# A decoder stack on one core: the third block of each MLP's first product by seven quarter products, with its weight sums on GpSimd

## The reference, cut to what matters

```python
def rms_norm(x, g):
    y = x * lax.rsqrt(jnp.mean(x * x, axis=-1, keepdims=True) + NORM_EPS)
    return y * g

def sqrelu_mlp(x, w1, w2):          # x 512 x 1024, w1 1024 x 4096, w2 4096 x 1024
    h = jax.nn.relu(x @ w1)
    return (h * h) @ w2
```

## Time and profile before

| | us |
|---|---|
| median of 3 runs | 1942.14 (1940.47 to 1942.18) |
| the profiled execution | 1938.0 |
| its span, first to last instruction | 1936.2 |
| TensorE busy | 1909.1 (99% of the span) |
| VectorE busy | 1364.7 (70%) |
| ScalarE busy | 913.6 (47%) |
| GpSimd busy | 243.6 (13%) |

### The profile page before, as it was taken

How to read it: one execution, slowest core, us unless ns; L and a number is a source line. 1 busy time by engine, 2 the same in 40 slices (tenths; PEclk the granted TensorE clock), 3 DMA queues, 4 the chain that set the end, 5 groups by cost and what they waited for, 6 DMA issues and landing times.

```text
span 1936.2 us, 29515 instructions
## 1 busy us (share of the span) xinstructions
PE 1909.1 (99%) x12066; PEld 1623.7 (84%) x12066; DVE 1364.7 (70%) x1899; ACT 913.6 (47%) x1366; POOL 243.6 (13%) x319
## 2 busy tenths in 40 slices
PE   9999999999999999999999999999999999999998
PEld 7877889899888876678899988887798788899897
DVE  5448587776775678857777776778765567777775
ACT  4227453433443688854343343676653444433432
POOL 3100000000002137620000000075400200000001
PEclk9999999999999999999999999999999999999999
DMA  6320223233234440013223223231143132233231
GB/s 205 103 92 3 88 90 107 87 110 109 88 109 131 151 132 2 2 45 109 88 90 114 102 87 112 90 109 55 53 144 132 44 109 88 88 109 109 88 109 66
DMA packets 30928, 181.36 MB, mean 94 GB/s; under 512 B 4752, under 2 KB 7824, under 8 KB 10320
## 3 DMA queue, kind: packets, MB, share of 16 engines
q1 hardware_dynamic: 28000, 172.68, 26.3%
q0 software_dynamic: 1952, 6.03, 1.1%
q10 hardware_dynamic: 848, 0.83, 0.1%
HBM read 172.72 MB, written 2.10 MB: 90 GB/s over the span
## 4 chain that ended last, share of the span: by engine, by line
PE 93%; DVE 3%; issue 1%; ACT 1%; POOL 1%; DMA 1%; DVEq 0%; POOLq 0%; ACTq 0%
PE ps L578 28%; PE ps L579 28%; PE ps L580 28%; PE ps L2017 2%; PE ps L1185 1%; PE ps L1975 1%; PE ps L1249 1%; PE ps L1225 1%; DVE n_probs L2121 1%; POOL f_probs L1907 1%; DVE f_probs L1798 0%; DMA x_res<-in_xT 0%; PE ps L1964 0%; PE ps L2014 0%; PE ps L1409 0%
## 5 line engine op out<-in xcount | busy, mean ns | idle before, releaser
L578 PE MATMUL ps<-o_hi,w_hi 128*128 128x512 f32 (+1 forms) x1032 | 403.4, 391 | 0.0
L579 PE MATMUL ps<-o_lo,w_hi 128*128 128x512 f32 (+1 forms) x1032 | 400.8, 388 | 0.0
L580 PE MATMUL ps<-o_hi,w_lo 128*128 128x512 f32 (+1 forms) x1032 | 400.3, 388 | 0.0
L547 ACT ACTIVATE w_hi<-w_raw 128x2048 fp32r<-128x2048 f32 x109 | 208.7, 1915 | 272.3 <-PE ps L580 271.3
L578 PE MATMUL ps<-h_hi,w_hi 128*128 128x512 f32 (+2 forms) x896 | 318.4, 355 | 1.5 <-DVE w_lo L557 0.9
L580 PE MATMUL ps<-h_hi,w_lo 128*128 128x512 f32 (+2 forms) x896 | 316.1, 353 | 0.0
L579 PE MATMUL ps<-h_lo,w_hi 128*128 128x512 f32 (+2 forms) x896 | 316.0, 353 | 0.0
L564 DVE TENSOR_TENSOR w_lo<-w_raw,w_hi 128x2048 fp32r<-128x2048 f32 x109 | 254.9, 2339 | 62.6 <-ACT w_hi L547 62.4
L580 PEld LDWEIGHTS ps<-o_hi,w_lo 128*128 128x128 f32 x1032 | 193.9, 188 | 40.1
L578 PEld LDWEIGHTS ps<-o_hi,w_hi 128*128 128x128 f32 x1032 | 194.0, 188 | 39.9 <-issue 1.5
L579 PEld LDWEIGHTS ps<-o_lo,w_hi 128*128 128x128 f32 x1032 | 194.1, 188 | 38.2 <-issue 0.5
(11 more groups left out here) (363 smaller groups left out, 3556.9 us busy)
## 6 DMA issues: line engine op xcount, KB each, us to landing
w_raw<-in_wstream SPq DMA_DIRECT2D x159, 1024.0 KB, 4.8
x_res<-in_xT SPq DMA_DIRECT2D x4, 512.0 KB, 4.6
out_T<-x_res SPq DMA_DIRECT2D x5, 256.0 KB, 2.4
e_cmp<-kv_nat POOLq DMA_DIRECT2D x8, 128.0 KB, 6.4
k_slc<-kv_nat POOLq DMA_DIRECT2D x8, 128.0 KB, 5.0
k_win<-kv_nat POOLq DMA_DIRECT2D x8, 128.0 KB, 7.5
mem_in<-in_memT POOLq DMA_DIRECT2D x1, 1024.0 KB, 5.1
e_cmp<-kv_nat POOLq DMA_DIRECT2D x8, 127.8 KB, 7.0
```

What stands on the lines that cost most here:

```text
L547: act.activation(w_hi[:, par, :, :], w_raw[:, par, :, :], ACT.Copy).then_inc(hi_ready, 1)
L578: pe.matmul(o, l_hi, r_hi, start=first, stop=False)
L579: pe.matmul(o, l_hi, r_lo, start=False, stop=False)
L580: return pe.matmul(o, l_lo, r_hi, start=False, stop=last)
```

## The change

Three things are changed, in each of the three MLPs.

1. `PLAIN` goes from 3 to 2, so slot 2 is a seven slot too. The order of hidden and output slots stays (`LEAD`, `PAIRED`).
2. For slot 2 alone, the four `sum_raw` sums (`raw_sums`) and the low parts of the plain quarters (`plain_lows`) are made by GpSimd in a new `pool_mlp`. GpSimd starts the sums when the block has landed, and the low parts when slot 0's tiles are done and ScalarE has made the high parts. VectorE keeps the two `sum_lo` subtractions of slot 2 and now waits for `plain_ready` ahead of the last.
3. The token work is earlier in the order. On VectorE `token_difference` stands ahead of `vector_root` in slot 0, `token_sums` ahead of the work on slot 2's weights, and `tokens_low` directly behind that, ahead of `hidden_low(0)` and of the evacuation of slot 1. On ScalarE `gained` is in slot 0, slot 2's `sums` ahead of `hidden(0)`, and `tokens_high` behind it, one slot earlier.

```diff
-        PLAIN = 3
+        PLAIN = 2
         SEVENS = 16 - PLAIN
...
+        LEAD, PAIRED = 3, 13
+        HIDDEN = {slot: slot for slot in range(LEAD)}
+        HIDDEN.update({LEAD + 1 + 2 * n: LEAD + n for n in range(PAIRED)})
+        OUTPUT = {LEAD + 2 * v: v for v in range(PAIRED)}
...
+        def raw_sums(eng, n, raw, begin, end):
+
+            if begin == 0:
+                eng.tensor_tensor(sum_raw[:, 0, :, :], quarter(1, 0, raw), quarter(1, 1, raw), ALU.add).then_inc(sums_made, 1)
+                eng.tensor_tensor(sum_raw[:, 1, :, :], quarter(1, 0, raw), quarter(0, 0, raw), ALU.subtract).then_inc(sums_made, 1)
+                eng.wait_ge(sums_made, 4 * n + 1)
+                eng.tensor_tensor(sum_raw[:, 2, :, :], sum_raw[:, 0, :, :], quarter(0, 0, raw), ALU.subtract).then_inc(sums_made, 1)
+            if end == 4:
+                eng.wait_ge(sums_made, 4 * n + 3)
+                eng.tensor_tensor(sum_raw[:, 3, :, :], quarter(0, 1, raw), sum_raw[:, 2, :, :], ALU.subtract).then_inc(sums_made, 1)
+
+        def plain_lows(eng, n, raw, hi, lo):
+
+            eng.wait_ge(plain_high, 2 * n + 1)
+            eng.tensor_tensor(lo[:, 4:8, :], raw[:, 4:8, :], f32(hi[:, 4:8, :]), ALU.subtract)
+            eng.wait_ge(plain_high, 2 * n + 2)
+            eng.tensor_tensor(quarter(0, 0, lo), quarter(0, 0, raw), f32(quarter(0, 0, hi)), ALU.subtract).then_inc(plain_ready, 1)
+
+        def pool_mlp(pool, m):
+
+            blk = b["mlp%d" % m] + LEAD - 1
+            par, n = blk % 2, SEVENS * m
+            raw, hi, lo = (w[:, par, :, :] for w in (w_raw, w_hi, w_lo))
+            pool.wait_ge(split_ready, blk - 1)
+            pool.wait_ge(raw_landed[par], 16 * (blk // 2) + 16)
+            raw_sums(pool, n, raw, 0, 4)
+            pool.wait_ge(tile_done, 2 * blk - 2)
+            plain_lows(pool, n, raw, hi, lo)
...
                 if slot == 0:
                     scalar_root(act, name)
+                    gained()
...
+                if slot == 1:
+                    sums(slot + 1)
                 if slot - 1 in HIDDEN:
                     hidden(slot - 1)
-                if seven(slot + 1):
+                if slot == 1:
+                    tokens_high()
+                if slot > 1 and seven(slot + 1):
                     sums(slot + 1)
                 if seven(slot):
                     copy_product(slot)
-                if slot == 1:
-                    gained()
-                if slot == 2:
-                    tokens_high()
...
+                if slot > LEAD - 1:
+                    dve.wait_ge(raw_landed[par], 16 * (blk // 2) + 16)
+                    dve.wait_ge(tile_done, 2 * blk - 2)
+                    raw_sums(dve, n, raw, 0, 3)
+                    plain_lows(dve, n, raw, hi, lo)
+                    raw_sums(dve, n, raw, 3, 4)
                 dve.wait_ge(sums_high, n + 1)
                 dve.wait_ge(sums_made, 4 * n + 4)
                 dve.tensor_tensor(sum_lo[:, 0:3, :, :], sum_raw[:, 0:3, :, :], f32(sum_hi[:, 0:3, :, :]), ALU.subtract)
                 dve.wait_ge(hi_ready, blk + 1)
+                dve.wait_ge(plain_ready, n + 1)
                 dve.tensor_tensor(sum_lo[:, 3, :, :], sum_raw[:, 3, :, :], f32(sum_hi[:, 3, :, :]), ALU.subtract).then_inc(split_ready, 1)
...
+                if slot == 1:
+                    token_sums()
                 if seven(slot + 1):
                     sums_and_lows(slot + 1)
                 elif blk + 1 < NBLK:
                     vector_split(dve, blk + 1, (blk + 1) % 2)
                 if slot == 0:
+                    token_difference()
                     vector_root(dve, name)
-                    token_difference()
+                if slot == 1:
+                    tokens_low()
                 if slot - 1 in HIDDEN:
                     hidden_low(slot - 1)
-                if slot == 1:
-                    token_sums()
-                if slot == 2:
-                    tokens_low()
...
             pool_sb(pool)
+            pool_mlp(pool, 0)
             pool_compress(pool)
             pool_nsa(pool)
+            pool_mlp(pool, 1)
...
             pool_cross(pool)
+            pool_mlp(pool, 2)
             pool_final(pool)
```

More of the change, by code:

```diff
@@ L799, in build_program @@
         SLOTS = 32
-        PLAIN = 3
+        PLAIN = 2
         SEVENS = 16 - PLAIN
-        HIDDEN = {slot: slot for slot in range(PLAIN)}
-        HIDDEN.update({PLAIN + 1 + 2 * n: PLAIN + n for n in range(SEVENS)})
-        OUTPUT = {PLAIN + 2 * v: v for v in range(SEVENS)}
+        LEAD, PAIRED = 3, 13
+        HIDDEN = {slot: slot for slot in range(LEAD)}
+        HIDDEN.update({LEAD + 1 + 2 * n: LEAD + n for n in range(PAIRED)})
+        OUTPUT = {LEAD + 2 * v: v for v in range(PAIRED)}
         LATE = {SLOTS - 3 + n: parts for n, parts in enumerate(LATE_PARTS)}
```

## The result

The changed kernel takes 1948.9 us (median of 6 runs, 1946.57 to 1950.65), the kernel before, run beside it, 1940.36 (6 runs, 1939.62 to 1942.18). The ratio is 1.0043, with 95% bounds of 1.0033 and 1.0053: it is 0.43% slower, against a forecast of 1948.2. But the forecast counted 6.1 us of loss from a median of 1942.14; the loss is 8.5, from 1940.36. So 2.4 us of the loss are not in the forecast's sum.

A forecast was written before the change was run, and what follows sets the result against it. TensorE, busy 99% of the span, bounds the kernel; per MLP 2.85 us late less 0.81 saved is 2.04, 6.1 for three; 1938.0 + 6.1 = 1944.1, plus 4.1 for the median gives 1948.2, range 1943 to 1952.

The forecast's parts named there:

- VectorE's chain: VectorE's queue in slot 1, from slot 0's evacuation to tokens_low: tok_ready at 267.82, wanted at 265.15.
- The restart: TensorE loading weights and starting again after its slot 2 wait: 0.2 us taken, 0 to 0.5.
- The hold-up: VectorE two-SBUF-input instructions and GpSimd's SBUF reads lock each other out; the two low parts cost VectorE 3.34 us.
- Rival A: Slot 2: no hold-up, or low parts done in time; TensorE gains 0.81 three times, median 1939.7; chance 0.12.
- B: Slot 2: GpSimd's turns cost VectorE half, 1.7 us; net 0.4 per MLP, 1943.3 in all; chance 0.15.
- C: GpSimd dearer, 1.86 and 3.72 us, so 5.20 lost; net 3.9 per MLP, 1953.8 in all; chance 0.11.
- That delay costs nothing more: GpSimd's sums delay slot 0's hid_buf to 254.2 from 252.64, without further cost, the low part lying partly under it.
- the lower one: Forecast's lower bound: GpSimd at 1.04 and 2.08, no restart; 2.25 late, net 1.24 per MLP, 1945.8.
- Later slots: From slot 3 on, the order slots 4, 5 and 6 have now, TensorE never idle; free.
- the 1.3 us to spare: Slot 3: hid_ready comes 5.9 us after tok_ready, while TensorE still has 7.2 us of matmuls.
- rival D: Stalled TensorE gets the lower clock for one slot per MLP, some 10 us more each, 1978; chance 0.02.
- The base: Median of the kernel before, 1942.14, 4.1 above its profiled execution of 1938.0; the forecast loss was added to it.

The follow-up runs named there:

- the table of two by two: Changed kernel with GpSimd's sums and low parts each kept or replaced by memsets; tok_lo ends 263.8 with neither, 267.0 low parts only, 265.4 sums only, 267.7 both.
- on VectorE: Changed kernel with slot 2's four sums and two low parts made by VectorE, no GpSimd work in the MLPs; 1958.88 us, 1.0101 of the kernel before.
- low parts twice: Changed kernel with GpSimd making slot 2's two low parts twice over; 1962.78 us, 1.0119 of the kernel before.
- the changed kernel again: Changed kernel run once more with no edit, for a second profile; 1949.22 us, 1.0041 of the kernel before.
- no reads: Changed kernel with GpSimd's six slot 2 instructions replaced by memsets of zeros, so it reads nothing; 1938.04 us, 0.999 of the kernel before.
- the sums alone: Changed kernel with GpSimd's four sums kept and its two low parts filled with zeros by memset; 1937.85 us, 0.9989 of the kernel before.
- token work early: Changed kernel with slot 2's products reordered, token_difference and gained before the previous layer's last tile, low parts on VectorE; 1937.07 us, 0.9985 of the kernel before.
- old product order: The token work early kernel with slot 2's products back in the changed kernel's order; 1940.81 us, 0.9999 of the kernel before.
- products reordered: Changed kernel with slot 2's seventh product taken third, ahead of those reading tok_hi and tok_lo; 1942.49 us, 1.0007 of the kernel before.
- low parts alone: Changed kernel with GpSimd's two low parts kept and its four sums filled with zeros by memset; 1947.23 us, 1.0034 of the kernel before.

## Why the prediction was right, and where it was not

**VectorE's chain** came out as worked out. On the scale of the earlier trace rows, predicted and measured: the split of slot 1 done at 247.3 and 247.05, `token_difference` at 249.6 and 249.3, the reciprocal 252.9 and 252.5, `hid_buf` of slot 0 at 254.2 and 253.9, `token_sums` 261.05 and 261.07, `sum_lo` 263.33 and 263.34, `tok_lo` 267.82 and 267.74, the third product 2.85 late and 2.65 (270.48 - 2.68 - 265.15). The restart was 0.06, not 0.2. Net 1.84 for each MLP where 2.04 was forecast; by the stretches between the MLPs 1.97.

**The hold-up**, read from one place in another stage, is the right mechanism: GpSimd's reads off, and it is gone; twice the low parts, and it is there twice. Rival A (no hold-up) falls with it, as does B (half): VectorE paid in full. The prices too: 2.41 for GpSimd's 1024 elements against 2.43; 3.2 us for the pair against 3.34. C (dearer with the rounded output) is out. The estimate of 2.25 from the Trainium skill (GPSIMD Engine Reference, Elementwise — side-by-side cycle accounting) was under the 2.41 that was measured. The reciprocal was taken as free, and that was not put to the test, since GpSimd has a gap there; what reads PSUM is free in the trace (1.29 for 1.28).

**"That delay costs nothing more"** was wrong. The delay from the sums costs 0.7 us of the final wait, shown by the table of two by two. The sum of the chain came out all the same, 267.74 for 267.82, and that is luck: without the sums `token_sums` starts 0.4 before the 252.64 that I had added to (252.2: `token_difference` no longer stands between the reciprocal and the evacuation), and the low parts cost a little less than I took. Of the bounds, the lower one has a slip: "2.25 late" should be 2.85 - 0.60 - 0.20 = 2.05, and its net of 1.24 follows from that.

**Later slots** were as predicted: no wait in slots 3 and 4, and the 1.3 us to spare showed when the first wait was taken away (1.20 of wait at slot 3).

**The mis-sized term is the clock, rival D.** I gave 0.02 to the lower clock, at a price of 10 us for each MLP. The mechanism was right and common, the price was off: 1.5 to 2.3 us a time, in none, two or all three MLPs of an execution. (The stretches between the MLPs grew by 6.76, 6.02 and 6.10 us in the kernel on VectorE, where the wait accounts for 4.44, and by 7.33, 7.78 and 7.17 with the low parts twice, where it accounts for 5.55.) Both grounds that I had against it fail on their own rows. A slice of the page is 48.4 us long and its digit 9 means 90% or more, so a drop for 3.4 us (271.2 to 274.6 in the changed kernel again) leaves it at 9; the page of the kernel with the low parts twice, with a drop in all three MLPs, has forty nines as well. And the "waits of several us in the attention stages" are totals of many short ones. In the list of the kernel before, the longest single wait of TensorE is 1.8 us:

```profile
PE ps L1975 <- DVE n_min L2121: 6.2, 9, 1.1
...
PE ps L384 <- DVE nrm L345: 1.8, 1, 1.8
```

So that trace held no wait like the one that I forecast, and said nothing about what follows one.

How much of the loss is the clock's can be worked out in two ways. The first goes by what the waits leave over. TensorE's lateness in slot 2 or 3 is the listed idle time plus 0.16 (the changed kernel's 2.65 against 2.49: the idle time starts at the modelled end of the last matmul, 0.28 long where they start every 0.12), so the waits of three MLPs make the sum of the three latenesses, less 2.4. The second way goes by the mean granted clock that is on record for every run of a kernel, not for the profiled one alone: (1 - granted clock) times the span is the time that the lower clock takes away, and the last column has its mean over the runs, less the same for the runs of before beside them.

| kernel | idle, three MLPs | from waits | measured | left over | by the granted clock |
|---|---|---|---|---|---|
| no reads | 0 | -2.4 | -2.8 | -0.4 | -0.6 |
| the sums alone | 0.5 | -1.5 | -3.0 | -1.5 | -1.4 |
| token work early | 0 | -2.4 | -3.5 | -1.1 | -0.4 |
| old product order | 1.8 | -0.1 | 0.0 | 0.1 | -0.6 |
| products reordered | 3.6 | 1.7 | 1.7 | 0.0 | -0.2 |
| low parts alone | 5.3 | 3.4 | 6.4 | 3.0 | 2.7 |
| changed kernel | 7.5 | 5.6 | 8.4 | 2.8 | 2.1 |
| on VectorE | 15.3 | 13.4 | 18.3 | 4.9 | 7.2 |
| low parts twice | 18.6 | 16.7 | 22.2 | 5.5 | 9.1 |

Waits of up to 1.2 us leave nothing over, or up to 1.5 us less than nothing; waits of 1.8 and more leave 3 to 5.5 us. The two last columns agree within 0.7 us down to the changed kernel. In the last two rows the recorded clock is also low for a part of the wait itself, where it costs nothing: that part is 2.6 and 4.4 us in the two profiles, and without it 4.6 and 4.7 are left, for 4.9 and 5.5. So about 2 to 3 us of the changed kernel's 8.4 are the lower clock. In the profiles it lies behind each of the waits of 1.8, 5.1 and 6.2 us (three of three in one execution of each kernel) and behind two of six of those of 2.5. It was not more frequent with the longer of 1.8 and 2.5; what decides whether it comes is open.

**The base** was off in the other direction. I took the median of three runs, 1942.14; the six runs beside the changed kernel give 1940.36, and 26 runs 1940.8. A loss 2.4 too small on a base 1.8 too high made 1948.2 against 1948.9. That it lies closer than its parts is luck. The 2.4 are 8.5 - 6.1: the waits came out at 5.6 by the sum above (5.9 by the stretches), and the rest, 2.6 to 2.9, is about what the lower clock takes. A gain of the size of TensorE's can be told from nothing, too: ten or eleven executions of a kernel showed 2.8 to 3.5 us, where I had taken 3.9 as the least.

## What to carry to other kernels

Work moved to an idle GpSimd isn't off VectorE where it reads SBUF beside VectorE's instructions with two SBUF inputs: each GpSimd turn costs VectorE about its length (3.2 us for turns of 3.7), and no wait in the trace says so, only longer instructions. Whether the move pays depends on what it lies beside. The low parts, wholly beside `token_sums`, cost VectorE 3.2 us for work that it does itself in 1.7. The sums, which lie partly where VectorE waits for others, cost it 0.7 to 1.6 us, for four instructions of 0.6 us each. Price such a move by where it lies; and before moving work at all, see whether the order of the consumer can ask for it later. With a TensorE that is never idle, count a new stall of about 2 us as its length plus, in some executions, 1.5 to 2.3 us for the lower clock; before calling such a cost absent, see whether your trace holds a single stall of that length, since a total of short ones and a digit of the page don't show it. And take the base from many runs.

## What the runs showed of the hardware

That a TensorE busy for 98% of the span is granted 1.2 GHz after a single short wait was not expected: 8.79 in place of 7.28 us for 60 matmuls after 2.5 us of idle time, in some executions and MLPs and not in others, with the drop coming 1.2 us after TensorE had started again (271.2 after 270.02); after 6.2 us the clock was low before it started. After waits of 0.75 and 1.20 us in the MLPs no profile has it; one of two profiles has it behind waits of 0.54 and 1.28 us that follow each other in the mixed attention layer.

A GpSimd subtraction to the rounded type, from quarters, took 2.41 us for 1024 elements, where 2.43 was estimated for a plain one; no plain one of that size was run. A plain one of 512 took 1.29 where nothing was beside it, the rounded one 1.48 beside `token_sums`. A memset of 1024 elements took 0.96, with nothing taken from VectorE.
